# Sliding attention: three pooling projections cut into halves over six units, pooling work in every second unit, attention halves of the output projection ahead of the pooled part

## The reference, cut to what matters

```python
def pool_mix(u, w_pool, pool_scale):          # u: 512 tokens x 512, four groups of 128
    for g, w in enumerate((2, 4, 8, 16)):
        mean = (csg[:, 1:] - csg[:, start]) / cnt[None, :, None]   # running mean over w tokens
        outs.append(mean - uf[:, :, lo:hi])
    d = jnp.stack(outs, axis=2).astype(u.dtype)
    y = jnp.einsum('bsgc,gcd->bsgd', d, w_pool).reshape(B, S, POOL_WIDTH)
    return y * pool_scale

def swa_with_sinks(q, k, v, sinks):           # 4 blocks of 128 queries, 2 KV heads, 4 heads each
    s = jnp.einsum('bnqkgd,bnjkd->bnkgqj', qb, kb) * (HEAD_DIM ** -0.5)
    s = jnp.where(valid[None, :, None, None], s, NEG_INF)
    p = jax.nn.softmax(jnp.concatenate([s, sink], axis=-1), axis=-1)[..., :-1]
    o = jnp.einsum('bnkgqj,bnjkd->bnqkgd', p.astype(v.dtype), vb)
    return o.reshape(B, S, ATTN_WIDTH)

def token_mixer(h, cos, sin, w_in, w_pool, pool_scale, sinks, g_pool, g_attn, w_out):
    z = h @ w_in                              # 1024 -> 512 pooled, 512 q, 128 k, 128 v
    pool_out = pool_mix(u, w_pool, pool_scale)
    attn_out = swa_with_sinks(q, k, v, sinks)
    y = jnp.concatenate([rms_norm(pool_out, g_pool), rms_norm(attn_out, g_attn)], axis=-1)
    return y @ w_out
```

## Time and profile before

| | |
|---|---|
| median of 3 runs | 1862.85 us (1860.32 to 1863.97) |
| the profiled execution's own time | 1865.49 us |
| its span | 1863.7 us |
| PE busy | 1804.5 us, 97% of the span |
| POOL, DVE, ACT busy | 1260.7, 783.8, 445.9 us |
| eight attention units, from unit 0's transposes to the first output half | 430.71 to 486.69 us of the span |

### The profile page before, as it was taken

One profiled execution on the slowest core, in us unless ns is written; L12 is line 12 of the kernel. 1 busy time (PEld: TensorE's weight loads), 2 busy tenths in 40 slices (PEclk: granted clock), 3 DMA queues, 4 the chain that ended last, 5 costly groups with the idle time before them and its releaser, 6 DMA issues.

```text
span 1863.7 us, 29319 instructions
## 1 busy us (share of the span) xinstructions
PE 1804.5 (97%) x11429; PEld 1435.9 (77%) x11429; DVE 783.8 (42%) x1401; ACT 445.9 (24%) x903; POOL 1260.7 (68%) x621
## 2 busy tenths in 40 slices
PE   8999999998899999999999999998889999999998
PEld 7888888876577888888777875666767888888887
DVE  5333360068475333300445344425646355555201
ACT  3000010045431000000322255544524231212000
POOL 8888887854259888877586442232466777877773
PEclk9999999999999999999999999999999999999999
DMA  5222233231023222233342531140024333332331
GB/s 187 101 91 101 94 94 100 80 108 67 23 68 102 101 101 90 94 94 106 127 176 97 164 127 60 45 159 14 4 95 174 94 98 93 98 98 90 94 98 60
DMA packets 60076, 180.32 MB, mean 97 GB/s; under 512 B 7203, under 2 KB 14243, under 8 KB 59084
## 3 DMA queue, kind: packets, MB, share of 16 engines
q1 hardware_dynamic: 49852, 164.71, 26.8%
q10 hardware_dynamic: 10128, 14.25, 2.2%
HBM read 165.81 MB, written 13.13 MB: 96 GB/s over the span
## 4 chain that ended last, share of the span: by engine, by line
PE 92%; DVE 3%; ACT 2%; issue 2%; DMA 0%; ACTq 0%; DVEq 0%
PE bank L567 25%; PE bank L569 25%; PE bank L568 25%; PE bank L993 1%; PE bank L1021 1%; PE bank L966 1%; PE bank L1182 1%; PE bank L585 1%; PE bank L589 1%; PE bank L586 1%; PE bank L928 1%; PE bank L1154 1%; PE bank L1167 0%; DMA x_tok<-x_dram 0%; DVE sc L2094 0%
## 5 line engine op out<-in xcount | busy, mean ns | idle before, releaser
L475 POOL TENSOR_TENSOR w_hi<-w_raw,one 128x1024 fp32r<-128x1024 f32 (+1 forms) x279 | 527.2, 1890 | 466.1 <-PE bank L569 406.0
L477 POOL TENSOR_TENSOR w_lo<-w_raw,w_hi 128x1024 fp32r<-128x1024 f32 (+1 forms) x279 | 682.7, 2447 | 21.9
L567 PE MATMUL bank<-h_hi,w_hi 128*128 128x512 f32 x1392 | 551.2, 396 | 4.7 <-DVE xT L1981 1.6
L568 PE MATMUL bank<-h_lo,w_hi 128*128 128x512 f32 x1392 | 542.7, 390 | 0.0
L569 PE MATMUL bank<-h_hi,w_lo 128*128 128x512 f32 x1392 | 542.7, 390 | 0.0
L567 PEld LDWEIGHTS bank<-h_hi,w_hi 128*128 128x128 f32 x1392 | 261.7, 188 | 66.5 <-issue 7.7
L568 PEld LDWEIGHTS bank<-h_lo,w_hi 128*128 128x128 f32 x1392 | 261.6, 188 | 57.1 <-issue 3.8
L569 PEld LDWEIGHTS bank<-h_hi,w_lo 128*128 128x128 f32 x1392 | 261.7, 188 | 55.0
L567 PE MATMUL bank<-a_hi,w_hi 128*128 128x512 f32 x528 | 205.5, 389 | 0.0
L569 PE MATMUL bank<-a_hi,w_lo 128*128 128x512 f32 x528 | 205.4, 389 | 0.0
L568 PE MATMUL bank<-a_lo,w_hi 128*128 128x512 f32 x528 | 205.4, 389 | 0.0
(11 more groups left out here) (394 smaller groups left out, 2175.4 us busy)
## 6 DMA issues: line engine op xcount, KB each, us to landing
w_raw<-w_ffn_gu_dram SPq DMA_DIRECT2D x88, 512.0 KB, 3.3
w_raw<-w_conv_up_dram SPq DMA_DIRECT2D x44, 512.0 KB, 3.5
w_raw<-w_ffn_down_dram SPq DMA_DIRECT2D x32, 448.0 KB, 3.2
w_raw<-w_ffn_down_dram SPq DMA_DIRECT2D x16, 512.0 KB, 3.5
w_raw<-w_out_dram SPq DMA_DIRECT2D x16, 512.0 KB, 3.4
w_raw<-w_gates_dram SPq DMA_DIRECT2D x16, 512.0 KB, 3.6
w_raw<-w_rwkv_dram SPq DMA_DIRECT2D x14, 512.0 KB, 3.4
w_raw<-w_conv_down_dram SPq DMA_DIRECT2D x16, 448.0 KB, 3.2
```

Source lines behind the costliest of these rows:

```text
L475: nc.gpsimd.tensor_tensor(w_hi[:, s, 0:width], raw, one[:, 0:1].to_broadcast([P, width]), ALU.mult).then_inc(sem("w_rounded"), 1)
L477: nc.gpsimd.tensor_tensor(w_lo[:, s, 0:width], raw, w_hi[:, s, 0:width].bitcast(F32), ALU.subtract).then_inc(sem("w_split"), 1)
L567: nc.tensor.matmul(dst, hi, rhs_hi[:, k, :], start=start and k == k0, stop=False)
L568: nc.tensor.matmul(dst, hi, rhs_lo[:, k, :], start=False, stop=False)
```

## The change

On PE the three whole chunks `mix_in(7)` to `mix_in(9)` behind units 0, 1 and 2 become six halves of 12 matmuls behind units 0 to 5 (`pool_half`). The first three pooling products move from behind units 3, 4, 5 to between `attend_window` and `sum_window` of units 2, 4, 6; the fourth moves from unit 6 to behind all units. Of the four sums of squares two stay ahead of the output projection, and one each follows the first and the second attention half. The wait for the last `pooled` moves from ahead of the output halves to ahead of the fourth.

On ACT `scale_probs` also takes units 5 and 6, and the squares of the third and fourth pooled tile move behind the four `h_hi` of the attention. On DVE only unit 7 is scaled, `pool_scaled` and `pool_difference` stand in units 0, 2, 4, 6, `pooled` in units 2, 4, 6 and, for the last, behind the four `h_lo` of the attention, and `normalise` stands ahead of `mask` in each unit.

```diff
--- before.py
+++ after.py
@@ -792,11 +792,24 @@
             rotate_q(3)
             units = [(n, g) for n in range(NT) for g in range(2)]
 
+            def pool_half(j, part):
+
+                c = FIRST["w_in"] + j
+                if part == 0:
+                    if j == 7:
+                        pe.wait_ge(*nth("z_read", 7))
+                    else:
+                        pe.wait_ge(*nth("pooled", j - 7))
+                last = chunk(c, c % RING, 4 * part, 4 * part + 4, h_hi, h_lo, bank[7][:, :], part == 0, part == 1, w0=0)
+                if part:
+                    last.then_inc(sem("w_used"), 1)
+
             def pool_product(i):
 
                 if i == 0:
                     pe.wait_ge(*nth("w_pool_in", 16))
-                    pe.wait_ge(*nth("z_read", 10))
+                if i < 3:
+                    pe.wait_ge(*nth("z_read", 8 + i))
                 else:
                     pe.wait_ge(*nth("pooled", i))
                 pe.wait_ge(*nth("pool_diff", i + 1))
@@ -814,16 +827,17 @@
                     attend_window(*units[u + 2], u + 2)
                 if u == 0:
                     pe.wait_ge(*nth("v_read", 1))
+                if u in (2, 4, 6):
+                    pool_product(u // 2 - 1)
                 sum_window(n, g, u)
-                if u < 3:
-                    mix_in(7 + u)
-                elif u < 7:
-                    pool_product(u - 3)
+                if u < 6:
+                    pool_half(7 + u // 2, u % 2)
 
             pe.wait_ge(*nth("swa_masked", 4 * len(units)))
-            sum_squares("pool", 4, "pool_in_sq", "pool_in_sq_used")
+            pool_product(3)
+            for k in range(2):
+                sum_square(k, 4, "pool_in_sq", "pool_in_sq_used", 0)
             pe.wait_ge(*nth("swa_out_read", len(units)))
-            pe.wait_ge(*nth("pooled", 4))
 
             def out_half(u, k0, begin=False):
 
@@ -832,7 +846,11 @@
                 return chunk(c, c % RING, k0, k0 + 4, h_hi, h_lo, bank[k0 + u % 4][:, :], True, True,
                              "wout_h_ready" if begin else None, w0=0, shift=-4 if k0 else 4)
             for u in range(4):
+                if u == 3:
+                    pe.wait_ge(*nth("pooled", 4))
                 out_half(u, 4, u == 0).then_inc(sem("wout_attn_post_sum"), 1)
+                if u < 2:
+                    sum_square(2 + u, 4, "pool_in_sq", "pool_in_sq_used", 0)
             for u in range(4):
                 if u == 2:
 
@@ -1518,7 +1536,7 @@
             exps(*units[1], 1)
             for u, (n, g) in enumerate(units):
                 copies(n, g, u)
-                if u < 4:
+                if u < 6:
                     scale_probs(*units[u + 1], u + 1)
                 if u == len(units) - 1:
                     pool_square(0)
@@ -1526,13 +1544,13 @@
                 store_out(n, g, u)
                 if u + 2 < len(units):
                     exps(*units[u + 2], u + 2)
-            pool_square(2)
-            pool_square(3)
 
             act.wait_ge(*nth("swa_out_read", len(units)))
             for k in range(4):
                 nc.scalar.activation(h_hi[:, 4 + k, :], mixed[:, 4 + k, :], ACT.Copy, scale=param("g_attn", k))\
                     .then_inc(sem("attn_h_hi"), 1)
+            pool_square(2)
+            pool_square(3)
             inv_rms("pool_in", "pool_in_sq_used", 4, 4 * P)
             round_h("pool", 0, 4)
             pre_norm_sums("attn", "swa_out_read", len(units), mixed, 4, 4, 3)
@@ -2110,7 +2128,7 @@
                 dve.wait_ge(*nth("swa_step", 2 * unit + 1))
                 nc.vector.reciprocal(sm[:, 3, :], sm[:, 3, :]).then_inc(sem("swa_step"), 1)
                 dve.wait_ge(*nth("swa_step", 2 * unit + 2))
-                if unit < 5:
+                if unit < 7:
                     return
                 for h in range(4):
                     nc.vector.tensor_scalar(sc[:, unit % 2, h, 0:width], sc[:, unit % 2, h, 0:width],
@@ -2121,20 +2139,19 @@
             mask(*units[1], 1)
             normalise(*units[1], 1)
             for u, (n, g) in enumerate(units):
-                if u < 4:
-                    pool_scaled(u)
-                else:
-                    pooled(u - 4)
-                if 1 <= u < 4:
+                if u % 2 == 0:
+                    pool_scaled(u // 2)
+                if 1 <= u < len(units) - 1:
                     normalise(*units[u + 1], u + 1)
                 if u + 2 < len(units):
                     mask(*units[u + 2], u + 2)
-                if 4 <= u < len(units) - 1:
-                    normalise(*units[u + 1], u + 1)
-                if u < 4:
-                    pool_difference(u)
+                if u in (2, 4, 6):
+                    pooled(u // 2 - 1)
+                if u % 2 == 0:
+                    pool_difference(u // 2)
             for k in range(4):
                 low_part("attn", "g_attn", k, mixed, 4, "wout_h_ready")
+            pooled(3)
             pre_norm("pool", "g_pool", "wout_h_ready", src=mixed, n=4, done=4)
 
             nc.vector.memset(acc[:, :], 0.0).then_inc(sem("wout_acc_zero"), 1)
```

## The result

The changed kernel took 1870.14 us in the median of 7 runs (1867.17 to 1872.58), the kernel before 1862.62 us (7 runs, 1859.05 to 1863.97): a ratio of 1.0044, 95% interval 1.0033 to 1.0056. The forecast was 1863.6 us and no change. Its likeliest case was wrong, its range to 1867.0 did not hold the time, and even the rival of three drops of the clock, 1866.9 us, was too fast.

The account below looks back on a forecast made before the run. PE was taken to bound the kernel. Waits -7.9 + 7.9, restarts +0.8 and clock -1.6 + 1.6 made +0.8 us, carried to the median: 1862.85 + 0.8 = 1863.6 us, range 1860.3 to 1867.0.

Parts of the forecast that it names:

- likeliest case: Whole kernel: the followed steps with one drop of the clock, 1863.6 us, no change; chance 0.3.
- rival of three drops of the clock: Attention units: stalls in unit 2, unit 4, units 6 and 7 each drop the clock; +4.0, 1866.9 us; chance 0.15.
- The bound and the place: PE bounds the kernel (92% of the chain); the change touches one stretch, the eight attention units.
- The waits: PE's waits, attention units through tail: 7.9 us removed, 7.9 us new, among them 2.75 in unit 2 and 1.7 in unit 4.
- Unit 7's scalings: Ahead of unit 7's transposes: scaling on DVE begins behind POOL's first instruction only, a PE wait of 0.55 us.
- Restarts: Projection begins six times instead of three, two squares cut output halves: five at 0.16, +0.8 us; ends 0 and 1.35.
- The clock: Attention units: old drop of 1.6 us goes, one new at unit 2's stall, 1.6; ends 0 and 4.8.
- rival B: Slower: stalls of unit 2, unit 4, units 6 and 7 each bring a clock drop; +4.0, 1866.9 us; chance 0.15.
- D: Unit 7's scalings wait for POOL's second instruction too, starting 2.2 us later; 1865.8 us, no change; chance 0.06.
- the prediction's own sign: Attention stretch: the prediction is wrong if the clock falls more than twice there.
- First output half: Start of the output projection: about 3 us earlier than 486.69 if the clock holds.
- first pooled half: Output projection, behind four attention halves: within 2 us of 497.6, where it stands before.

Follow-up runs that it names:

- e4: Kernel before with only the tail change: squares 3 and 4 behind attention halves, and ACT's order with it; 1863.67 us, ratio 1.0004 to the kernel before.
- e2: Changed kernel, but POOL splits chunk 3 of the output projection only behind unit 7's scaled probabilities; 1865.78 us, ratio 1.0015 to the kernel before.
- e3: Changed kernel with 24 extra unread 128x512 matmuls ahead of the third and fifth projection halves and unit 7's transposes; 1862.52 us, ratio 0.9998 to the kernel before.
- e11: The kernel before, untouched, profiled once more; 1861.46 us for the single execution, attention stretch 160.01 us.
- e7: Changed kernel with ACT scaling unit 7's probabilities as well; 1864.26 us, ratio 1.0016 to the kernel before.
- e14: Changed kernel with 24 extra unread matmuls ahead of the third and fifth halves and unit 7's transposes, only 8 columns wide; 1868.50 us, ratio 1.0021 to before.
- e1: Changed kernel, but POOL splits output chunks 1, 2, 3 behind the first pooled tile, the second, and unit 7's scaled probabilities; 1866.57 us, ratio 1.0022 to before.
- e15: Changed kernel with `pooled` ahead of the mask (units 2, 4), ACT scaling unit 7, 15 extra matmuls plus ten of 8 columns; 1858.07 us, 0.9969 of before.

## Why the prediction was wrong, point by point

**The bound and the place** held: PE is the chain, the stretch is where the loss is made, and `e4` shows that its part of the tail is free.

**The waits** were followed rightly but for one. The new ones for `pooled` were put at 2.75 and 1.7 us and are 2.5 and 1.15, the reason, `normalise` behind POOL's instructions, as forecast. ACT's scaling of units 5 and 6 is no bound: no long wait appeared in units 3 and 5. The total was put at no change and rose by 1.1 us, from 10.5 to 11.6.

**Unit 7's scalings**, the first step that failed: "their scaling on DVE begins behind POOL's first instruction", 0.55 us of wait. They wait for the second as well, 2.3 us. The argument against it was a misreading: 0.285 us for 256 elements is faster than the mask's 1.74/4 = 0.435, not as slow, so the pace spoke for nothing. The price in wait is 1.7 us; it had a chance of 0.06. The Trainium skill, "SBUF — State Buffer", section "Who interferes with whom", says that `tensor_scalar` and `copy` can take the ports that DVE and GpSimd share, and that the later instruction then waits for the whole of the earlier. This case's trace agrees: 3.10 us against 1.14 for the scalings, and in `e2` a copy of 1.68 against 0.41.

**Restarts** were put at 0.8. With the clock full the stretch is 161.47 (`e3`) against 160.01 (`e11`), 1.5 us; less 1.1 of waits leaves 0.4.

**The clock** is the term that decided: "-1.6 + 1.6". The drop was priced well, 1.6 against 1.7 us. Its number was not. The changed kernel has a single and a double drop in the stretch, 5.1 us, in both of its profiles; the one taken away, 1.7 us, is not there in every execution of the kernel before, so less than 1.7 can be set against it. The two failures are one chain: the scalings' wait of 2.3 us, which the sum priced at 0.55, is what brings the double drop, since `e7`, which shortens that wait alone, has none there. A stall of 2.75 us was seen as the one risk, and rival B, with three drops at the three stalls, had the right mechanism, but stood at 0.15 and without D. That its 4.8 us are near the 5.1 is in part luck: no drop came at unit 4, and the one at unit 7 was of double length. So the prediction's own sign, more than two drops in the stretch, did not show. B and D together make 1866.9 + 2.2 = 1869.1 us, near what came, again with luck, since 1.8 us of the loss to the clock lie outside the stretch. Treating them as apart was the error of the chances.

**First output half.** Forecast at about 3 us earlier than 486.69; it came at 490.15. Less 1.65 of shift from ahead of the stretch, the 4.1 that the drops cost by then (`e3`) and 1.7 of unit 7's wait, that is 482.7, where the forecast for a clock that holds was about 483.7. The first pooled half was to stand within 2 us of 497.6 and stood at 503.30; less the same, 495.9. So the unit-by-unit steps were right to 1 or 2 us, and these two things were laid on top.

**What stays open.** Of the 6.1 us lost to the clock the stretch explains 4.3 (5.1 less the mean, 0.85, of 1.7 and nothing). The other 1.8 are drops outside. They come at fixed places of the program (near 991, 1086, 1277, 1365 and 1390 us) in some executions: four each in the changed kernel's two profiles between the stretch and the end, four and one in the two of before. (A drop at the very end, in all 17 profiles, is left out.) Two profiles each can't tell whether the change has a part in that. Nor is it only the changed kernel: `e3` loses 7.0 us to the clock in the mean with no drop in the stretch of its profile. The drop at 7 to 11 us is there in three of 17 profiles of all kinds, and belongs to none of the edits.

## What to carry to other kernels

A wait of the engine that bounds is not paid by its length alone. Here the two empty waits of 2.5 and 2.3 us cost 1.4 and 2.6 us again in slow matmuls behind them, so some 6 us of waiting is cheaper as five waits of 1.2 us than with two of 2.4 among them; where one can't be avoided, matmuls that nobody reads give the clock's part back.

A small DVE step that other engines wait for belongs behind no GpSimd instruction: look for a wait between the two in each place it is moved to, and give scalings whose input and output are both in SBUF to ACT where GpSimd works beside them.

A gain of a few microseconds from an edit that adds or removes instructions needs a control with the same instructions at the same places that lacks only the effect in question: 25 matmuls of 8 columns gave 3.9 us that had looked like the clock's.

## What the runs showed of the hardware that was not expected

Drops of the clock in these stages come in one length or in two: 1.7 us lost behind the waits for `pooled`, 3.4 behind the scalings' wait, where a second wait of 1.17 us follows at the lower clock. In `e7`, with waits of 0.87 and 1.17 there, none came. In `e14`, with 1.06 (behind ten matmuls of 8 columns) and 1.17, the double one came, and behind unit 2, with 1.28 behind ten such, none. In `e1` the double one followed a wait of 2.5 us with no second wait behind it, so the second wait is not what doubles it; `e15` has one far from the stretch, at 1377 to 1384 us. What doubles a drop is open.

Ten matmuls of 8 columns took 1.28 us, 0.13 each, and ten of 512 took 2.57: here 8 columns cost half of what 512 cost.

The same instructions behind the stretch took between 1317.2 and 1324.4 us in 17 profiles, through drops of the clock and through issue gaps of 4.3 to 10.8 us in one stage.
